# The last stage of a two-block network: half of a gather behind the first weight chunk, four scatter products split two and two

## The chip, the cores and the metric

One core of one Trainium2 chip. The time is that of the device from the first to the last instruction of the program, in microseconds (us). Names of engines: TensorE (PE in the profile; PEld is its weight load), VectorE (DVE), ScalarE (ACT), GpSimd (POOL), SyncE (SP), which here issues the weight transfers. 16 DMA engines move all data between the memory and the core.

## The reference, cut to what matters

The program runs a first block of two layers (mixers, cross attention, MLP) and then a second block. The change lies in the last part of the second, an expert-choice feed-forward network with 16 experts, each of which takes the 64 tokens of 512 that it rates highest:

```python
def expert_choice_ffn(h, w_router, b_router, w_gate, w_up, w_down):
    cap = (EC_CAPACITY_FACTOR * S) // N_EXPERTS          # 2 * 512 // 16 = 64
    affinity = jax.nn.softmax((h @ w_router + b_router).astype(jnp.float32), axis=-1)
    gates, idx = lax.top_k(affinity.transpose(0, 2, 1), cap)
    xin = h[bidx, idx]
    hid = jax.nn.silu(jnp.einsum('becd,edf->becf', xin, w_gate)) * jnp.einsum('becd,edf->becf', xin, w_up)
    y = jnp.einsum('becf,efd->becd', hid, w_down) * gates[..., None].astype(h.dtype)
    return jnp.zeros_like(h).at[bidx, idx].add(y)
...
x = x + gate2 * expert_choice_ffn(h2, w_router[l], b_router[l], w_gate[l], w_up[l], w_down[l])
```

The model width is 1024, an expert's inner width 2048, and everything is float32. The three weights of 16 experts are 403 MB.

## The kernel before, in words

Each engine has its own program, written out by hand; engines meet only at semaphores (`wait_ge`, `then_inc`), and an engine does its instructions in the order of its program. Where a text below says that something is queued behind a wait, that order is meant.

**Closing the mixer** (`close_parts`, from line 2480). The last output projection, the row scales, the router's logits and the ranks of the tokens are made. VectorE ends it with `hot` (L2717), a 0/1 matrix of tokens by slots for the first two experts, and signals `hot_ready`.

**The expert stage** (`experts`, from line 2724) works on experts in pairs, eight of them. Expert 0 of a pair uses columns 0 to 63 of TensorE's array and expert 1 columns 64 to 127. The weights come in chunks of 2048 KB (four blocks of 128 input features, 512 output columns, both experts), 24 for each pair: `per = 4 * nf + 8`, for each of the four quarters of the inner width two of the gate weight and two of the up weight, then eight of the down weight. The chunks of all pairs go through eight slots in turn (`slots`): four called ring, three in second_arena, one in hT. The first eight are loaded while the mixer is being closed. For every further chunk j SyncE waits until TensorE is through with chunk j - 8 (`tiles_done`) and then issues its load (L2785, L2786), in the order of the chunks.

On TensorE a pair is:

- `gather` (L2843): with `hot` it picks the 64 tokens of each expert out of `h2`, features in rows: 32 products of 128 columns, in two halves `q` of four feature blocks each, into bank 4 and bank 5; each half signals `s_gat`. VectorE moves each half to `xc` (`move_gathered`, L2929 to L2935, four instructions) and signals `s_x`.
- `pair_of_groups` (L2811): two chunks, with eight products each. Chunk q = 0 needs the first half of `xc`, q = 1 the second. In the first group of a pair TensorE waits for `s_x` ahead of each chunk (L2816).
- between the groups, one of the eight `scatter` products of the pair before (L2859), which bring its rows back to the tokens; for the first pair they work on zeros.
- turns of the hidden values, then the down projection, whose four groups are b = 0 (kg = 0, 1) for output columns 0 to 511 and b = 1 (kg = 0, 1) for 512 to 1023. The gather of the next pair comes after b = 0 (L2891).

The first pair's gather is called ahead of the loop (L2895), both halves in a row. The pairs 0 to 6 run in a loop (`Fori`), the last is written out.

**The end.** The last pair has no next pair under which its scatter products could go. The four of output half c = 0 are called by `scatter_half(0)` after kg = 0 of b = 1 (L2888, L2889), when two chunks are left; the four of c = 1 by `scatter_half(1)` at the very end (L2899). Each waits on `s_y`: VectorE has to multiply the down projection's result by gate2 first (L2981). VectorE's program for b = 0 and b = 1 is this, and it stays as it is:

```python
for b in range(2):
    dve.wait_ge(g.tiles_done, i * per + (base + 4 * nf + 4 * b + 4))
    nc.vector.tensor_tensor(y[:, b * BANK:b * BANK + BANK], g.psum[:, 6 + b, :],
                            gate2[:, b * BANK:b * BANK + BANK], ALU.mult).then_inc(s_y.up(), 1)
    if last:
        add_half(b)
```

`add_half(c)` (L2945) is four additions, one for each block of 128 tokens, each of which waits for its scatter product. SyncE and ScalarE write each finished block to the output (L2803, L2923). The last chunk of all is loaded in two halves (L2799), with a semaphore of its own for the second.

Of the kernel before, what the change touches and what calls it, by code (L numbers as in the profile page):

```python
# [12 lines left out]
P = 128  # L13
SEQ = 512
NT = SEQ // P
# [2708 lines left out]
def experts(g, ya, late, mod, gate2, out):  # L2724


    nc, t = g.nc, g.t
    pairs, nf = EXPERTS // 2, FE // BANK
# [20 lines left out]
    def preload(sp, which):  # L2749
        for s in which:  # L2750
# [4 lines left out]
    rows_ready, hot_ready, ya_turned, logits_done = opening[5:]  # L2755
    base = g.tiles
    primed = [g.counter("ex_" + n).up() for n in names for _ in range(2)]
    s_gat, s_x, s_silu, s_hid, s_turn, s_copy, s_y, s_back, s_add = (g.counter("ex_" + n) for n in names)
    all_primed = g.counter("built")
    s_gated, s_slots = g.counter("ex_slots_gated"), g.counter("ex_slots_turned")  # L2760
    xc, sg, y, h2, hot, gated, slot, aff, pos = (late[n] for n in ("xc", "sg", "y", "h2", "hot", "gated", "slot", "aff",
                                                                   "pos"))
# [3 lines left out]
    with nc.Block() as block:  # L2766
# [41 lines left out]
        def _(pe):  # L2808
            opening[2](pe)

            def pair_of_groups(i, j, bank, lhs, start, stop, halved=False, gathered=False):  # L2811

                for q in range(2):
                    w = ring[(j + q) % slots].rearrange("p (e k n) -> p e k n", e=2, k=half)
                    if gathered:
                        pe.wait_ge(s_x.sem, i * 2 + (s_x.base + q + 1))  # L2816
                    pe.wait_ge(landing[(j + q) % slots], i * (16 * per // slots) + landed_at[j + q])
                    for k in range(half):
                        if halved and q == 1 and k == half // 2:
                            pe.wait_ge(half_landed, 16)  # L2820
                        first, last = start and q == k == 0, stop and q == 1 and k == half - 1
                        for e in range(2):
                            mm = nc.tensor.matmul(g.psum[64 * e:64 * e + 64, bank, :],  # L2823
                                                  lhs(q * half + k)[:, 64 * e:64 * e + 64], w[:, e, k, :],
                                                  start=first, stop=last)
                    mm.then_inc(g.tiles_done, 1)
# [10 lines left out]
            def turn_slots(i):  # L2837
# [2 lines left out]
                    mm = nc.tensor.transpose(g.psum[:, 4, tt * P:tt * P + P], gated[:, tt, :], g.ident[:])  # L2840
                mm.then_inc(s_slots.up(), 1)

            def gather(i):  # L2843

                pe.wait_ge(hot_ready.sem, i + (hot_ready.base + 1))
                for q in range(2):
                    for k in range(4 * q, 4 * q + 4):
                        for tt in range(NT):
                            mm = nc.tensor.matmul(g.psum[:, 4 + q, (k % 4) * P:(k % 4) * P + P],  # L2849
                                                  h2[:, tt, k * P:k * P + P], hot[:, tt, :],  # L2850
                                                  start=(tt == 0), stop=(tt == NT - 1))
                    mm.then_inc(s_gat.up(), 1)

            def scatter(i, u):

# [3 lines left out]
                nc.tensor.matmul(g.psum[:, 6 + u % 2, :], sg[:, tt * P:tt * P + P], y[:, c * BANK:c * BANK + BANK],  # L2859
                                 start=True, stop=True).then_inc(s_back.up(), 1)  # L2860

            def scatter_half(c):

                pe.wait_ge(s_y.sem, (pairs - 1) * 2 + (s_y.base + c + 1))
                for tt in range(NT):
                    nc.tensor.matmul(g.psum[:, last_banks[c][tt], :], sg[:, tt * P:tt * P + P],  # L2866
                                     y[:, c * BANK:c * BANK + BANK], start=True, stop=True).then_inc(s_back.up(), 1)

            def pair(i, last):
                pe.wait_ge(s_y.sem, i * 2 + s_y.base)  # L2870
                for b in range(nf):
                    if b >= 2:
                        pe.wait_ge(s_hid.sem, i * nf + (s_hid.base + b - 1))
                    pair_of_groups(i, 4 * b, (b % 2) * 2, lambda k: xc[:, k, :], True, True, gathered=(b == 0))
                    scatter(i, 2 * b)
                    pair_of_groups(i, 4 * b + 2, (b % 2) * 2 + 1, lambda k: xc[:, k, :], True, True)
                    scatter(i, 2 * b + 1)
                    if b:
                        turn(i, b - 1)
                turn(i, nf - 1)  # L2880
                pe.wait_ge(s_copy.sem, i * nf + (s_copy.base + nf))
                turn_slots(i)
                pe.wait_ge(s_add.sem, i * 2 * NT + (s_add.base + 2 * NT))
                for b in range(2):
                    for kg in range(2):
                        pair_of_groups(i, 4 * nf + 4 * b + 2 * kg, 6 + b, lambda k: hT[:, kg * KD + k, :],
                                       kg == 0, kg == 1, last and b == kg == 1)
                        if last and b == 1 and kg == 0:  # L2888
                            scatter_half(0)  # L2889
                    if b == 0 and not last:  # L2890
                        gather(i + 1)  # L2891

            pe.wait_ge(*all_primed.at(1))
            pe.wait_ge(*rows_ready.at(NT))
            gather(0)  # L2895
            with pe.Fori(0, pairs - 1) as i:
                pair(i, False)
            pair(pairs - 1, True)
            scatter_half(1)  # L2899

        @block.scalar
# [192 lines left out]
```

## Time and profile before

| | us |
|---|---|
| median of 3 runs | 3101.69 |
| lowest and highest run | 3094.66 and 3102.46 |
| the profiled execution | 3105.4 |
| its span in the profile | 3103.7 |
| TensorE busy | 2888.8 (93%) |
| VectorE busy | 778.7 (25%) |
| ScalarE busy | 442.2 (14%) |
| mean DMA rate over the span | 184 GB/s |
| expert stage, from the first gather product (2173.17) to the end | 930.5 |

How to read the rows below. All times are us from the start of the span; a duration "mean ns" is in ns. In a **timeline** a row is: start, duration, engine, line of the kernel, operation, what it writes <- what it reads, shapes, count merged into the row, and in brackets the idle time of the engine before it and what ended that. Ends of products are modelled, so a row can end 0.1 us after the next one's start. TensorE does each float32 product in two passes, so a count is twice the number of products. In the **chain of waits** a row is: start, duration, and the engine, transfer or line that the end of the program hung on in that time. In a **table of stretches** a row is: from and to, length, busy us of PE, PEld, DVE, ACT and POOL with their instructions in brackets, the granted TensorE clock (1.00 is 2.4 GHz, 0.50 is 1.2 GHz), the busy share of the 16 DMA engines, and GB/s.

### The profile page before, as it was taken

The numbers are of one execution on the slowest core, as the hardware profiler recorded it, in microseconds if no ns is written. First come the engines' busy times: TensorE is split into PE (matmuls) and PEld (weight loads), VectorE is DVE, ScalarE is ACT, GpSimd is POOL, SyncE is SP. The second block draws the span as 40 slices with busy tenths as digits, with TensorE's granted clock in tenths as the row PEclk, the third lists the DMA queues.
The fourth block names the chain that finished last, engine by engine and source line by source line (L and its number), as shares of the span: only waits on it lengthen the run. The fifth ranks groups of instructions, "written<-read, shape, count | busy, mean of one in ns | idle before, by whom it ended". The sixth has DMA issues, their size and how long they took to land. (4 is left out here: it accounts for less than half of the span.)

```text
span 3103.7 us, 25172 instructions
## 1 busy us (share of the span) xinstructions
PE 2888.8 (93%) x9875; PEld 1323.0 (43%) x9875; DVE 778.7 (25%) x2032; ACT 442.2 (14%) x934; POOL 56.7 (2%) x149
## 2 busy tenths in 40 slices
PE   8998889999999999999999899798999899899888
PEld 4544544444444445444544444464433233233232
DVE  3398523101001214240000244544111111111111
ACT  2123412100001003211000122242000000000000
POOL 0000000000000000110000010000000000000000
PEclk9998999999999999999999999898999999999999
DMA  7230011212222111582112111213899999999998
GB/s 274 68 109 14 1 40 54 83 61 75 81 82 84 56 54 55 174 282 102 65 64 72 54 56 55 75 39 126 346 427 428 428 429 429 428 428 428 429 427 375
DMA packets 107475, 570.75 MB, mean 184 GB/s; under 512 B 11578, under 2 KB 12364, under 8 KB 82940
## 3 DMA queue, kind: packets, MB, share of 16 engines
q1 hardware_dynamic: 99248, 538.64, 43.2%
q0 software_dynamic: 6768, 29.43, 2.8%
q10 hardware_dynamic: 1372, 1.51, 0.1%
q8 instruction: 56, 0.92, 0.1%
q14 instruction: 31, 0.25, 0.0%
HBM read 567.43 MB, written 6.32 MB: 185 GB/s over the span
## 5 line engine op out<-in xcount | busy, mean ns | idle before, releaser
L205 PE MATMUL banks<-hT,ring 128*128 128x512 f32 x1024 | 441.5, 594 | 5.1 <-PEq L298 5.1
L205 PEld LDWEIGHTS banks<-hT,ring 128*128 128x128 f32 x1024 | 195.0, 191 | 250.4 <-issue 250.4
L2823 PE MATMUL banks<-ring,second_arena 128*64 128x512 f32 x1024 | 232.0, 597 | 29.7 <-DMA ring<-in_w_up 16.0
L1890 PE MATMUL banks<-ring,second_arena 128*128 128x512 f32 x512 | 222.6, 597 | 0.0
L324 PE MATMUL banks<-ring,m_u 128*128 128x512 f32 x512 | 220.3, 592 | 1.6 <-PEq L178 1.6
L2823 PE MATMUL banks<-second_arena 128*64 128x512 f32 x768 | 174.5, 598 | 17.4 <-DMA second_arena<-in_w_gate 15.0
L1890 PEld LDWEIGHTS banks<-ring,second_arena 128*128 128x128 f32 x512 | 98.2, 192 | 123.0 <-issue 123.0
L324 PEld LDWEIGHTS banks<-ring,m_u 128*128 128x128 f32 x512 | 97.0, 190 | 123.4 <-issue 123.4
L2823 PEld LDWEIGHTS banks<-ring,second_arena 128*64 128x64 f32 x1024 | 70.0, 136 | 184.0 <-issue 133.5
L2823 PE MATMUL banks<-ring,mod 128*64 128x512 f32 x512 | 114.7, 596 | 13.1 <-DMA ring<-in_w_down 13.1
L2943 DVE TENSOR_TENSOR x_rows<-banks,x_rows 128x512 f32<-128x512 f32 x64 | 44.2, 691 | 282.4 <-PE banks L2859 282.4
L1655 PE MATMUL banks<-hT,ring 128*128 128x512 f32 x256 | 112.1, 600 | 2.6 <-PEq L298 2.6
L1422 PE MATMUL banks<-ring,hT 128*128 128x512 f32 x256 | 111.1, 595 | 0.9 <-PEq L786 0.9
L2823 PEld LDWEIGHTS banks<-second_arena 128*64 128x64 f32 x768 | 51.2, 136 | 133.3 <-issue 89.6
L2823 PE MATMUL banks<-second_arena,mod 128*64 128x512 f32 x384 | 84.6, 595 | 2.5 <-DMA second_arena<-in_w_down 2.5
L2972 DVE TENSOR_TENSOR mod<-banks,mod 128x512 f32<-128x512 f32 x32 | 22.1, 691 | 244.4 <-PE banks L2823 244.4
L360 ACT ACTIVATE x_square<-x_rows 128x1024 f32<-128x1024 f32 x20 | 21.2, 1058 | 398.5 <-DVE x_rows L348 217.1
L1805 DVE SCALAR_TENSOR_TENSOR mod<-second_arena,mod 128x1536 f32<-128x1536 f32 x32 | 58.2, 1818 | 75.8 <-DMA second_arena<-in_w_ada 75.7
L1655 PEld LDWEIGHTS banks<-hT,ring 128*128 128x128 f32 x256 | 49.1, 192 | 64.1 <-issue 64.1
L1422 PEld LDWEIGHTS banks<-ring,hT 128*128 128x128 f32 x256 | 48.7, 191 | 62.0 <-issue 61.2
L2823 PE MATMUL banks<-hT,second_arena 128*64 128x512 f32 x256 | 58.3, 597 | 14.9 <-DMA hT<-in_w_up 14.9
L2859 PE MATMUL banks<-second_arena 128*128 128x512 f32 x128 | 72.0, 645 | 0.0
(578 smaller groups left out, 3027.7 us busy)
## 6 DMA issues: line engine op xcount, KB each, us to landing
ring<-in_w_up SPq DMA_DIRECT2D x48, 2048.0 KB, 30.7
ring<-in_w_down SPq DMA_DIRECT2D x48, 2048.0 KB, 33.8
ring<-in_w_gate SPq DMA_DIRECT2D x32, 2048.0 KB, 34.0
second_arena<-in_w_gate SPq DMA_DIRECT2D x32, 2048.0 KB, 30.7
second_arena<-in_w_down SPq DMA_DIRECT2D x24, 2048.0 KB, 35.4
second_arena<-in_w_up SPq DMA_DIRECT2D x16, 2048.0 KB, 32.4
hT<-in_w_up SPq DMA_DIRECT2D x16, 2048.0 KB, 33.8
second_arena<-in_w_ada POOLq DMA_DIRECT2D x32, 768.0 KB, 4.8
```

What stands on the lines that cost most here:

```text
L205: mm = nc.tensor.matmul(o, w[:, k, a:z], src[:, ka, 0:ntok], start=(ka == 0), stop=(ka == kc * kgroups - 1))
L324: mm = nc.tensor.matmul(g.psum[:, b * NT + m, :], act[:, ka, m * P:m * P + P], w[:, k, :], start=(ka == 0), stop=(ka == kc * kgroups - 1))
L360: g.alink(nc.scalar.activation(square[:], g.x[:, t, :], ACT.Square, accum_out=g.row_stats[:, 0, t:t + 1]))
L1422: mm = nc.tensor.matmul(bank, a[:, k, m * P:m * P + P], w[:, k, :], start=(k == 0), stop=(k == kc - 1))
L1655: mm = nc.tensor.matmul(o, w[:, k, m * P:m * P + P], g.hT[:, k, :], start=(k == 0), stop=(k == KD - 1))
L1805: nc.vector.scalar_tensor_tensor(o, w[:, n % 2, :], cs[:, k:k + 1], o, ALU.mult, ALU.add).then_inc(added.up(), 1)
L1890: mm = nc.tensor.matmul(g.psum[:, b * NT + m, :], u[:, ka, m * P:m * P + P], w[:, k, :], start=(ka == 0), stop=(ka == KD * kgroups - 1))
L2823: mm = nc.tensor.matmul(g.psum[64 * e:64 * e + 64, bank, :], lhs(q * half + k)[:, 64 * e:64 * e + 64], w[:, e, k, :], start=first, stop=last)
L2859: nc.tensor.matmul(g.psum[:, 6 + u % 2, :], sg[:, tt * P:tt * P + P], y[:, c * BANK:c * BANK + BANK], start=True, stop=True).then_inc(s_ba ...
L2943: nc.vector.tensor_tensor(xs, g.psum[:, 6 + u % 2, :], xs, ALU.add).then_inc(s_add.up(), 1)
L2972: nc.vector.tensor_tensor(hid[:, b % 2, :], g.psum[:, (b % 2) * 2 + 1, :], act_g[:, b % 2, :], ALU.mult).then_inc(s_hid.up(), 1)
```

## The change

Two edits, both in TensorE's program. The other engines' programs are as before.

1. The gather is cut into `gather_half(q)`. The first pair is taken out of the loop and written out. Ahead of it only `gather_half(0)` is done; `gather_half(1)` comes inside its first group, after the products of chunk 0 and ahead of the wait for the second half of `xc`. Pairs 1 to 6 run in the loop as before, and their gathers are as before.
2. In the last pair, `scatter_half(0, ...)` is called twice: token blocks 0 and 1 after kg = 0 of b = 1 and token blocks 2 and 3 after kg = 1, that is after the last chunk.

```diff
                 for q in range(2):
                     w = ring[(j + q) % slots].rearrange("p (e k n) -> p e k n", e=2, k=half)
+                    if gathered and q and isinstance(i, int) and i == 0:
+                        gather_half(1)
                     if gathered:
                         pe.wait_ge(s_x.sem, i * 2 + (s_x.base + q + 1))
                     pe.wait_ge(landing[(j + q) % slots], i * (16 * per // slots) + landed_at[j + q])
...
+            def gather_half(q):
+                for k in range(4 * q, 4 * q + 4):
+                    for tt in range(NT):
+                        mm = nc.tensor.matmul(g.psum[:, 4 + q, (k % 4) * P:(k % 4) * P + P],
+                                              h2[:, tt, k * P:k * P + P], hot[:, tt, :],
+                                              start=(tt == 0), stop=(tt == NT - 1))
+                mm.then_inc(s_gat.up(), 1)
+
             def gather(i):
 
                 pe.wait_ge(hot_ready.sem, i + (hot_ready.base + 1))
                 for q in range(2):
-                    for k in range(4 * q, 4 * q + 4):
-                        for tt in range(NT):
-                            mm = nc.tensor.matmul(g.psum[:, 4 + q, (k % 4) * P:(k % 4) * P + P],
-                                                  h2[:, tt, k * P:k * P + P], hot[:, tt, :],
-                                                  start=(tt == 0), stop=(tt == NT - 1))
-                    mm.then_inc(s_gat.up(), 1)
+                    gather_half(q)
...
-            def scatter_half(c):
+            def scatter_half(c, tiles=range(NT)):
 
                 pe.wait_ge(s_y.sem, (pairs - 1) * 2 + (s_y.base + c + 1))
-                for tt in range(NT):
+                for tt in tiles:
...
-                        if last and b == 1 and kg == 0:
-                            scatter_half(0)
+                        if last and b == 1:
+                            scatter_half(0, (2 * kg, 2 * kg + 1))
                     if b == 0 and not last:
                         gather(i + 1)
 
             pe.wait_ge(*all_primed.at(1))
             pe.wait_ge(*rows_ready.at(NT))
-            gather(0)
-            with pe.Fori(0, pairs - 1) as i:
+            pe.wait_ge(*hot_ready.at(1))
+            gather_half(0)
+            pair(0, False)
+            with pe.Fori(1, pairs - 1) as i:
                 pair(i, False)
             pair(pairs - 1, True)
             scatter_half(1)
```

## Rows read from the trace of the kernel before

**Rows 1.** Table of stretches, the first and a late 100 us of the stage.

```profile
2182.00:2282.00 100.00, 99.19 (x474) 38.03 (x475) 14.97 (x28) 5.95 (x9) 0.00 (x0) 1.00 0.96 405
2982.00:3082.00 100.00, 85.51 (x366) 26.70 (x364) 9.68 (x14) 5.95 (x9) 0.00 (x0) 1.00 1.01 428
```

**Rows 2.** Chain of waits, where it turns to the transfers, and one round.

```profile
2334.25 32.40 DMA ring<-in_w_down
2366.69 3.68 PE banks L2823 x16
2370.39 35.44 DMA ring<-in_w_up
2405.87 3.68 PE banks L2823 x16
```

**Rows 3.** Timeline of the opening: gather, its two moves, first products.

```profile
2173.17 9.27 PE L2849 MATMUL banks<-second_arena 128*128 128x128 f32 x64 [1.46 <-DVE second_arena L2717]
2179.01 1.37 DVE L2933 TENSOR_SCALAR second_arena<-banks,mod_columns 128x128 f32<-128x128 f32 x4 [5.98 <-PE banks L2849]
2182.37 7.09 PE L2823 MATMUL banks<-ring,second_arena 128*64 128x512 f32 x32
2182.48 1.36 DVE L2933 TENSOR_SCALAR second_arena<-banks,mod_columns 128x128 f32<-128x128 f32 x4 [2.10 <-PE banks L2849]
```

**Rows 4.** Timeline of SyncE's queue: the first, the second and the third refill.

```profile
2186.07 0.33 SPq L2786 DMA_DIRECT2D ring<-in_w_gate  x1
2189.50 0.33 SPq L2786 DMA_DIRECT2D ring<-in_w_gate  x1
2194.14 3.76 SPq L2786 DMA_DIRECT2D ring<-in_w_up  x2
```

**Rows 5.** Table of stretches, single microseconds: clock, and bytes after the first refill.

```profile
2177.00:2178.00 1.00, 1.00 (x10) 1.00 (x10) 0.00 (x0) 0.00 (x0) 0.00 (x0) 0.94 0.00 0
...
2186.00:2187.00 1.00, 1.00 (x8) 0.29 (x5) 0.00 (x0) 0.00 (x0) 0.00 (x0) 1.00 0.00 0
2187.00:2188.00 1.00, 1.00 (x6) 0.29 (x4) 0.00 (x0) 0.00 (x0) 0.00 (x0) 1.00 1.16 246
2188.00:2189.00 1.00, 1.00 (x8) 0.29 (x4) 0.00 (x0) 0.00 (x0) 0.00 (x0) 1.00 0.82 344
```

**Rows 6.** Timeline of the second pair's gather and its first move.

```profile
2264.06 7.41 PE L2849 MATMUL banks<-second_arena 128*128 128x128 f32 x64
...
2267.93 1.36 DVE L2933 TENSOR_SCALAR second_arena<-banks,mod_columns 128x128 f32<-128x128 f32 x4 [3.07 <-PE banks L2849]
```

**Rows 7.** Timelines of TensorE, then VectorE, in the last 25 us.

```profile
3081.69 3.65 PE L2823 MATMUL banks<-second_arena,mod 128*64 128x512 f32 x16 [1.24 <-DMA second_arena<-in_w_down]
3085.27 3.70 PE L2866 MATMUL banks<-second_arena 128*128 128x512 f32 x8
3088.90 3.65 PE L2823 MATMUL banks<-second_arena,mod 128*64 128x512 f32 x16
...
3096.78 3.70 PE L2866 MATMUL banks<-second_arena 128*128 128x512 f32 x8 [0.79 <-DVE second_arena L2981]
...
3086.44 0.69 DVE L2950 TENSOR_TENSOR x_rows<-banks,x_rows 128x512 f32<-128x512 f32 x1 [10.15 <-PE banks L2866]
3087.29 0.69 DVE L2950 TENSOR_TENSOR x_rows<-banks,x_rows 128x512 f32<-128x512 f32 x1 [0.17 <-PE banks L2866]
...
3096.04 0.69 DVE L2981 TENSOR_TENSOR second_arena<-banks,mod 128x512 f32<-128x512 f32 x1 [6.34 <-PE banks L2823]
```

**Rows 8.** Timeline of TensorE: two pauses of earlier stages.

```profile
462.65 15.67 PE L1103 MATMUL banks<-hT,ring 128*128 128x512 f32 x32 [2.55 <-PEq L298]
...
1787.62 27.70 PE L2083 MATMUL banks<-hT,ring 128*128 128x512 f32 x64 [1.67 <-PEq L1848]
```

**Rows 9.** Table of stretches, around and behind these two pauses.

```profile
1786.00:1790.00 4.00, 2.38 (x6) 1.22 (x7) 1.69 (x4) 1.07 (x2) 0.00 (x0) 1.00 0.72 218
463.00:468.00 5.00, 5.00 (x9) 2.06 (x8) 1.82 (x12) 0.00 (x0) 0.00 (x0) 0.66 0.54 207
```

## The prediction

> **What bounds the kernel now.** The change touches two places, the opening of the expert stage and its last 20 us, so I read first what connects them. In the table of 100 us stretches the 16 DMA engines are full from the first expert chunk to the last: 428 GB/s at a share of 1.01 near the end, and 405 GB/s in the first stretch, which is what is left of 428 if nothing moves for its first 5 us [rows 1]. In the chain of waits the stage is one pattern, 3.68 us of products, then 35.44 us of a transfer, again and again [rows 2]: a slot is released, its new chunk is queued behind seven others, lands, and is used. One round is 2405.87 - 2366.69 = 39.18 us for eight slots, so 39.18 / 8 = 4.90 us per chunk of 2048 KB, 428 GB/s. TensorE needs less: two chunks in a row are 3.43 us apart and with a scatter product between them 4.64 us [rows 4]. So the **weight stream sets the end**. It starts when the first of the eight preloaded slots is released, and whatever moves its start, or makes a hole in it, moves the end by as much. A hole elsewhere on TensorE costs nothing while it has chunks in store. At the very end the order turns round: after the last chunks have landed TensorE, VectorE and the write of the output are in line, and there each microsecond counts again.
>
> The sum is made against the profiled execution, 3105.4 us with a span of 3103.7. That is 3.7 us above the median of the runs, 3101.69; I carry the difference over to the median. The runs themselves lie 7.8 us apart (3094.66 to 3102.46), more than anything below. About 0.3%, 9.3 us, is what a measurement of this kernel can tell from no change.
>
> **The opening, part by part.** Before: both halves of the gather start at 2173.17 and take 9.27 us; VectorE moves the first half from 2179.01 for 1.37 us, under the second half, and the first chunk starts at 2182.37 without waiting for anything [rows 3]. SyncE issues the first refill at 2186.07, that is 3.70 us later, and the second at 2189.50 [rows 4].
>
> After, the first half still ends for VectorE at 2179.01 (the clock's cold part lies all in it: 0.94 is granted in the microsecond from 2177 [rows 5], and the change touches nothing ahead of that). Now nothing lies beside the move: 2179.01 + 1.37 = 2180.38, a hand-over of 0.07, first chunk at 2180.45, its release and the first refill at 2180.45 + 3.70 = **2184.15, 1.92 us earlier**. This is the gain, and it is real.
>
> Then the second half of the gather stands on TensorE between chunk one and chunk two. At full clock a half costs what it costs in the second pair, 3.87 us from the start of the gather to VectorE's first move [rows 6]; starting at about 2183.98 it is there at 2187.85. The move behind it takes 1.36 us and is now bare as well (before it ran under the first chunk): 2189.21, hand-over 0.07, second chunk at 2189.28, second refill at 2189.28 + 3.70 = **2192.98, 3.48 us later** than before.
>
> What does the stream make of that? Before, the second transfer was queued at 2189.50 but its turn came only when the first was through, as if issued at 2186.07 + 4.90 = 2190.97; the 1.47 us between were cover. After, the first transfer is alone and is through at the equivalent of 2184.15 + 4.90 = 2189.05, and the second is issued at 2192.98. The engines stand idle for 3.9 us, and the second and every later chunk is 2192.98 - 2190.97 = **2.0 us later**. The early refill gives one chunk a head start and takes it back from all the others. The third refill follows 4.64 us after the second [rows 4], at 2197.62, against a need at 2192.98 + 4.90 = 2197.88: 0.26 us of cover, then more with each chunk (3.43 and 4.64 in turn against 4.90). So there is one hole and not a row of them. After a pause the engines also have to get going again: no bytes in the microsecond after the first refill's issue, 246 GB/s in the next and 344 in the one after it [rows 5]. The latency to the first byte is the same in both kernels and cancels; of the ramp I add the last part, (428 - 344) / 428 = 0.2 us; its bounds are 0 and 0.6 us (with the 246 as well). It can't be below nothing, since a transfer that starts from rest isn't faster than one in a full queue. **Opening: +2.2 us, between +1.9 and +2.8.**
>
> The rest of the opening is free. TensorE is about 3.5 us later through the first pair, which only eats into its store of landed chunks: the chain is on TensorE until 2334 and goes to a transfer only there, 150 us on [rows 2]. If that store were gone, it would cost these 3.5 us. The first pair leaves the loop and stands as straight code; its instructions are as many, and entry to the loop moves to a place with the same cover. Queued on VectorE behind its longer wait for the second half is the gating of the slots, which is needed only after all sixteen up and gate chunks. On SyncE nothing is moved but the times of the issues.
>
> **The tail.** Before, TensorE finishes the last but two chunk, does the four products of the first output half (3085.27 to 3088.90, so 3.63 us: 1.06 for the first and 0.857 for each further), then the last two chunks, after which VectorE multiplies (3096.04) and the second four products start at 3096.78 [rows 7]. The weights' own time would be earlier: chunk 190 lands 4.90 us after chunk 189, whose products start at 3081.69, so at 3086.59, and is used at 3088.90.
>
> After, only two products stand before the last two chunks: 2 x 0.857 = 1.71 us less, chunk 190 starts at 3087.19, still 0.6 us behind its landing. The last group ends 1.71 us earlier and the two remaining products start where its successor would stand. VectorE follows a last product by 0.11 (2182.37 to 2182.48 [rows 3]), so that place was 3096.04 - 0.11 = 3095.93 and is 1.71 less now, 3094.22. But VectorE works in the order of its program, and that isn't changed: all four additions of the first half, and only then the multiplication of the second half, on which the last four products wait. The first addition starts 3086.44 - 3085.27 = 1.17 us after the first product [rows 7], so the third addition now starts at 3095.39, the fourth 0.85 later (3086.44 to 3087.29) at 3096.24, ends 0.69 later at 3096.93, and the multiplication starts there instead of at 3096.04. Everything behind it (0.7 us multiplication, products, additions, a write) is as before. **Tail: +0.9 us.** The 1.7 us of product time are taken off the path ahead of the last chunks, and 1.17 + 0.85 + 0.69 = 2.7 us of product and additions are put on it behind them. What can add: the last chunk has to land up to 1.7 us earlier than it was wanted, and the output writes of the first half (128 x 512 floats, 256 KB, 0.6 us each at 428 GB/s) share the engines with it; two of the four are now behind it. I put that at 0, with a bound of +0.5. Nothing in the order on VectorE leaves room below +0.9.
>
> **Sum: 2.2 + 0.9 = +3.1 us.** The profiled execution would be 3108.5, the median 3101.69 + 3.1 = **3104.8 us**, which is within 0.3%.
>
> **The rivals.** *The gains stand.* The head start of 1.92 us would reach the end if the second refill came by 2189.05, and the tail would gain if the multiplication weren't behind the additions: the last products would then start when the two before them are through, at 3094.22 + 1.06 + 0.86 = 3096.14 instead of 3096.78, 0.64 us earlier. Together -2.6 (1.92 + 0.64), 3099.1 us. Against it stand the 3.87 + 1.36 us between the chunks and the order in the code; for it only that landing and issue times may be looser than I read them. 7%.
>
> *The clock falls in the new pauses* (the case that ends clearly slower). TensorE is idle for 1.6 us before the first chunk and for 1.4 us before the second. Rows on both sides: after a pause of 1.67 us the granted clock stayed at 1.00, its upper level of 2.4 GHz, while after one of 2.55 us the next 5 us ran at 0.66 on the mean [rows 8, 9], which is (1 - 0.66) x 5 = 1.7 us lost. New pauses are nearer to the first. One fall puts the second refill 1.7 us later, two 3.4: +4.8 or +6.5, 3106.5 to 3108.2 us; 7%. It would pass 9.3 us only if the clock stayed at 0.50 for both chunks and the half between them, 3.6 + 3.6 us more and so +10.3, 3112 us; 2%. The Trainium skill (TensorE: Matmul & The Clock Gate, HAM oscillation) speaks against this change here: bursts of products with pauses between them can throw the clock back to half rate again and again. By that rule the time would be the dearer of these cases; the row of 1.67 us is why I don't take it.
>
> *The change does nothing*: the stream's start doesn't set the end, say because a later place refills the queue. 3101.7 us, give or take the tail. The table of stretches shows no gap in which the stream could be caught up [rows 1]; 4%.
>
> **How the numbers follow.** Forecast 80%, and the rivals 7, 7, 2 and 4%. The costs themselves span +2.8 to +4.2 us (1.9 + 0.9 to 2.8 + 1.4); the wider part of the range is from the runs, whose median may fall 4 us to either side, and more below, where one run of before lies 7 us under the two others. 3097.5 to 3109.5 us takes in every case but the last clock case. Faster by over 0.3% would need a median under 3092.4: 2%. Slower by over 0.3%, above 3111: the full clock case and an unlucky spread, 4%. Within 0.3%: 94%.
>
> **What would show it.** In the changed kernel's trace: first refill 1.9 us earlier after the start of the gather and second 3.5 us later; a pause without bytes of 3 to 4 us between them; chunk-to-chunk times of 4.90 as before; the whole stage from the start of the gather to the last chunk's products some 2.2 - 1.7 = 0.5 us longer; at the end two additions between the last group and the multiplication, which starts 2.7 us after that group instead of at once. Wrong is the prediction if the engines are busy through the pause, if the clock reads under 1.00 at 2180 to 2193, or if the multiplication comes ahead of the third addition.

## The result

The changed kernel takes 3107.22 us, median of 21 runs (3098.27 to 3109.96), against 3103.01 us for the kernel before in the 21 runs beside it, which include the three shown above. The ratio is 1.0019 with a 95% interval of 1.0011 to 1.0027, that is 3.4 to 8.4 us: a little slower, by less than the 0.3% that is told from no change here. The forecast was 3104.8 us, +3.1.

The profiled execution has a span of 3106.9 us, 3.2 above the 3103.7 of before. Its chain of waits, at the opening and at the end (start, duration, what the end of the program hung on):

```profile
2172.79 5.70 PE banks L2848 x32
2178.48 1.61 issue
2180.09 3.65 PE banks L2825 x16
2183.75 3.78 PE banks L2848 x32
2187.88 1.05 DVE second_arena L2940 x3
2188.97 3.65 PE banks L2825 x16
...
3084.11 3.65 PE banks L2825 x16
3087.76 1.91 PE banks L2871 x4
3089.68 7.02 PE banks L2825 x32
3096.69 1.93 PE banks L2871 x4
3098.65 0.69 DVE x_rows L2957
3099.34 0.61 DVE second_arena L2988
3099.99 3.71 PE banks L2871 x8
```

Lines have moved: L2825 is the product of a weight chunk (L2823 before), L2848 the gather, L2871 the scatter of the last pair, L2957 and L2988 the addition and the multiplication on VectorE. Beside [rows 3] a pause now follows each half of the gather, and the second half stands between two chunks. Beside [rows 7] there is an addition between the last group of products and the multiplication.

SyncE's queue, the first three refills:

```profile
2183.78 0.33 SPq L2786 DMA_DIRECT2D ring<-in_w_gate  x1
...
2192.67 0.33 SPq L2786 DMA_DIRECT2D ring<-in_w_gate  x1
2197.31 0.33 SPq L2786 DMA_DIRECT2D ring<-in_w_up  x1
```

Counted from the first gather product (2173.17 before, 2172.79 now), the first refill comes at 10.99 instead of 12.90 us and the second at 19.88 instead of 16.33 [rows 4]. The hole between them in the table of stretches, by single microseconds (the last three columns are clock, share of the DMA engines, GB/s):

```profile
2184.00:2185.00 1.00, 1.00 (x11) 1.00 (x10) 0.00 (x0) 0.00 (x0) 0.00 (x0) 1.00 0.73 164
2185.00:2186.00 1.00, 1.00 (x11) 1.00 (x10) 0.00 (x0) 0.00 (x0) 0.00 (x0) 1.00 0.67 180
2186.00:2187.00 1.00, 1.00 (x11) 1.00 (x10) 0.00 (x0) 0.00 (x0) 0.00 (x0) 1.00 1.00 426
...
2190.00:2191.00 1.00, 1.00 (x8) 0.32 (x6) 0.00 (x0) 0.00 (x0) 0.00 (x0) 1.00 0.05 16
2191.00:2192.00 1.00, 1.00 (x6) 0.29 (x4) 0.00 (x0) 0.00 (x0) 0.00 (x0) 1.00 0.06 16
2192.00:2193.00 1.00, 1.00 (x5) 0.30 (x2) 0.00 (x0) 0.25 (x1) 0.00 (x0) 1.00 0.00 0
2193.00:2194.00 1.00, 1.00 (x4) 0.20 (x4) 0.19 (x1) 1.00 (x1) 0.00 (x0) 1.00 0.87 180
2194.00:2195.00 1.00, 1.00 (x8) 0.33 (x6) 0.50 (x1) 0.63 (x2) 0.00 (x0) 1.00 0.54 197
2195.00:2196.00 1.00, 1.00 (x8) 0.39 (x6) 0.00 (x0) 0.00 (x0) 0.00 (x0) 1.00 0.95 410
```

The first transfer goes through alone, then three microseconds move next to nothing, and a second start from rest follows. These stretches are cut at whole microseconds and not at the issue, so they can't be set beside [rows 5]. Counted from the issue, the first two microseconds of each start are these: first the kernel before, then the first and the second start of the changed kernel.

```profile
2186.07:2187.07 1.00, 1.00 (x6) 0.29 (x4) 0.00 (x0) 0.00 (x0) 0.00 (x0) 1.00 0.40 82
2187.07:2188.07 1.00, 1.00 (x8) 0.35 (x6) 0.00 (x0) 0.00 (x0) 0.00 (x0) 1.00 0.76 164
...
2183.78:2184.78 1.00, 1.00 (x9) 1.00 (x10) 0.00 (x0) 0.00 (x0) 0.00 (x0) 1.00 0.34 82
2184.78:2185.78 1.00, 1.00 (x11) 1.00 (x10) 0.00 (x0) 0.00 (x0) 0.00 (x0) 1.00 1.02 246
...
2192.67:2193.67 1.00, 1.00 (x4) 0.24 (x5) 0.00 (x0) 0.92 (x1) 0.00 (x0) 1.00 0.35 82
2193.67:2194.67 1.00, 1.00 (x7) 0.43 (x8) 0.69 (x1) 0.96 (x2) 0.00 (x0) 1.00 0.79 180
```

Each start has the same two slow microseconds, and the third is at 426, 328 and 393 GB/s. TensorE is busy through nearly the whole hole (1.00 in each microsecond from 2190): nothing in its own row would tell that anything is lost there. The clock reads 1.00 on both sides of the new pauses.

### The profile page after: what moved, and what is told of

It is laid out like the page before. It is cut to its first block and busy times, and to the rows that moved or that the text cites. A ratio compares the mean times of both kernels' runs of the same rounds, so it can differ in the third digit from the quotient of the medians.

```text
span 3106.9 us, 25150 instructions
## 1 busy us (share of the span) xinstructions
PE 2889.2 (93%) x9875; PEld 1324.9 (43%) x9875; DVE 778.2 (25%) x2032; ACT 442.2 (14%) x934; POOL 57.2 (2%) x149
## 3 DMA queue, kind: packets, MB, share of 16 engines
q10 hardware_dynamic: 1372, 1.51, 0.2%
## 5 line engine op out<-in xcount | busy, mean ns | idle before, releaser
L2825 PE MATMUL banks<-ring,second_arena 128*64 128x512 f32 x1024 | 232.2, 598 | 32.8 <-DMA ring<-in_w_up 16.0
L2825 PE MATMUL banks<-second_arena 128*64 128x512 f32 x768 | 174.5, 598 | 17.3 <-DMA second_arena<-in_w_gate 15.0
L2825 PEld LDWEIGHTS banks<-ring,second_arena 128*64 128x64 f32 x1024 | 70.1, 136 | 186.6 <-issue 134.5
L2825 PE MATMUL banks<-ring,mod 128*64 128x512 f32 x512 | 114.7, 596 | 12.4 <-DMA ring<-in_w_down 12.4
L2825 PEld LDWEIGHTS banks<-second_arena 128*64 128x64 f32 x768 | 51.2, 136 | 133.2 <-issue 89.9
L2825 PE MATMUL banks<-second_arena,mod 128*64 128x512 f32 x384 | 84.6, 595 | 2.5 <-DMA second_arena<-in_w_down 2.5
L2825 PE MATMUL banks<-hT,second_arena 128*64 128x512 f32 x256 | 58.3, 597 | 14.9 <-DMA hT<-in_w_up 14.9
```

The source lines that it names most:

```text
L2825: mm = nc.tensor.matmul(g.psum[64 * e:64 * e + 64, bank, :], lhs(q * half + k)[:, 64 * e:64 * e + 64], w[:, e, k, :], start=first, stop=last)
```

## How the experiments are read

Runs of one and the same kernel lie some 12 us apart (3093.66 to 3105.69 for the kernel before), far more than the terms in question. One reason shows long ahead of the stage. A pause of TensorE and the 7 us from its end, in the kernel before:

```profile
1005.38 7.08 PE L1655 MATMUL banks<-hT,ring 128*128 128x512 f32 x12 [2.55 <-PEq L298]
...
1005.40:1012.40 7.00, 7.00 (x13) 3.02 (x14) 3.31 (x17) 0.00 (x0) 0.60 (x16) 0.76 0.54 192
```

and the same place in e10 below, a second execution of the same kernel:

```profile
1002.92 7.11 PE L1655 MATMUL banks<-hT,ring 128*128 128x512 f32 x16 [2.55 <-PEq L298]
...
1003.00:1010.00 7.00, 7.00 (x18) 3.17 (x19) 3.26 (x17) 0.00 (x0) 0.54 (x15) 1.00 0.54 193
```

Behind the same pause of 2.55 us the clock fell in one execution (0.76 over 7 us, so (1 - 0.76) x 7 = 1.7 us lost) and not in the other. Of the thirteen traces here five have the fall at this place and eight don't. The kernel before has it at the like pauses at 556 and 1184 us as well (0.77 over 7 us each), and e10 at neither. Mostly by such falls the two executions of one kernel are 2173.17 - 2168.60 = 4.57 us apart by the start of the gather. So each trace is split at that start. **A** is from the first gather product to the start of the products of the last chunk but two (3081.69 - 2173.17 = 908.52 before), **B** from there to the end of the last addition (3101.21 - 3081.69 = 19.52). Between, the refills are counted from the first gather product too; there are 184, and the numbers below are the difference to the kernel before at the 1st, 2nd, 61st, 171st and last one. Worked out from the rows of SyncE's queue and of TensorE:

```
                       refill 1      2     61    171    184       A        B
before                     0.00   0.00   0.00   0.00   0.00   908.52   19.52
e10 before again          -0.16  -0.15  -0.18  -0.19  -0.19   908.33   19.52
after                     -1.91  +3.55  +2.85  +2.78  +2.80   911.32   20.31
e9  after again           -1.92  +3.54  +1.96  +1.88  +3.10   911.61   20.31
e1  opening alone         -1.92  +3.55  +2.50  +2.48  +3.64   912.16   19.53
e8  written out alone     -0.16  -0.16  -0.40  -0.39  +0.81   909.41   19.52
e4  short half            -1.92  +0.87  +0.08  +0.06  +0.31   908.85   19.53
e5  double half           -1.92  +7.11  +6.65  +6.61  +7.06   915.59   19.53
e6  four firsts           -2.06  -2.06  -2.49  -2.48  -0.91   907.59   19.53
e2  end alone             -0.02  -0.02  -0.15  -0.23  -0.21   908.31   20.31
e3  end mended            -0.02  -0.01  -0.10  -0.14  -0.14   908.40   18.65
e7  both mended           -2.06  -2.05  -2.37  -2.37  -0.91   907.60   18.66
e11 both mended again     -1.91  -1.91  -2.24  -2.23  -0.76   907.76   18.66
```

B repeats to 0.01 us for each form of the end. The stream's position repeats to 0.4 us for the kernels with no hole, and to 0.9 for those with one.

## The two edits alone

**e1** has the opening of the changed kernel and the end of the one before:

```diff
-                        if last and b == 1:
-                            scatter_half(0, (2 * kg, 2 * kg + 1))
+                        if last and b == 1 and kg == 0:
+                            scatter_half(0)
```

> The opening as changed (half of the gather behind the first chunk, first pair written out), the end as before. Measured in the trace as two stretches: A from the start of the first gather product to the start of the products of the last chunk but two (908.5 us before, 911.3 with the whole change), and B from there to the end of the last addition (19.5 before, 20.3 with the whole change). Stream theory (a hole in the weight stream is paid at the end in full): A 911.3, B 19.5, so 2.8 us above the kernel before. Rival 1 (the head start is kept and the loss is made elsewhere, in the end): A 906.6, B 19.5, 1.9 us below. Rival 2 (the two edits cost more together than alone, since the writes of the output meet the last chunk): A 911.3 but B under 19.5 or over 20.

A 912.16, B 19.53; ratio 1.0010 (0.9998 to 1.0023). The loss is in A as the stream theory has it, and B is that of before, so the head start isn't kept and the edits don't meet. Up to refill 171 it is +2.5. The rest, 1.15 us, comes in one jump at refill 173, which no theory had foreseen; it has a section of its own below.

**e2** is the kernel before with the split scatter products alone (`scatter_half` takes the token blocks as in the change).

```diff
...
-                        if last and b == 1 and kg == 0:
-                            scatter_half(0)
+                        if last and b == 1:
+                            scatter_half(0, (2 * kg, 2 * kg + 1))
```

> The end as changed (two scatter products before the last two chunks, two behind), the opening as before. Stretch A 908.5, B 20.3 (+0.8) if VectorE's order is the cost: the second multiplication starts 2.7 us behind the start of the two late products. Rival (the end costs nothing by itself and its 0.8 us come from the late stream): A 908.5, B 19.5 or less.

A 908.31, B 20.31; ratio 1.0006 (0.9996 to 1.0016). The whole +0.8 of the end is there without the late stream.

**e3** keeps that split and gives VectorE the order that would suit it:

```diff
...
                     if last:
-                        add_half(b)
+                        add_half(0, (2 * b, 2 * b + 1))
+                    if last and b == 1:
+                        add_half(1)
```

(with the multiplication of b = 1 ahead of it, and `add_half` taking the token blocks it is to add).

> As the run with the end alone, and VectorE's order changed too: two additions, then the second multiplication, then the other two additions and the last four. Theory (the cost of the end is VectorE's order, not the products): the multiplication starts 0.1 us behind the last group again, the last four products follow the two late ones without a pause, B is 19.5 - 0.65 to 19.5 - 0.85 = 18.7 to 18.9. Rival (the last chunk's landing is what ends last once the products are out of the way): the last group ends no earlier than before and B stays at 19.5 or above.

B 18.65, inside what was expected, if at its favourable edge; ratio 1.0002 (0.9992 to 1.0012), so the gain shows in the trace alone. The timeline of its end:

```profile
3090.14 3.60 PE L2823 MATMUL banks<-hT,mod 128*64 128x512 f32 x16
3093.67 5.42 PE L2866 MATMUL banks<-second_arena 128*128 128x512 f32 x12
3093.79 0.69 DVE L2981 TENSOR_TENSOR second_arena<-banks,mod 128x512 f32<-128x512 f32 x1 [6.33 <-PE banks L2823]
3094.83 0.69 DVE L2950 TENSOR_TENSOR x_rows<-banks,x_rows 128x512 f32<-128x512 f32 x1 [0.35 <-PE banks L2866]
```

and the changed kernel's:

```profile
3093.09 3.60 PE L2825 MATMUL banks<-hT,mod 128*64 128x512 f32 x16
3096.62 1.98 PE L2871 MATMUL banks<-second_arena 128*128 128x512 f32 x4
3097.79 0.69 DVE L2957 TENSOR_TENSOR x_rows<-banks,x_rows 128x512 f32<-128x512 f32 x1 [7.38 <-PE banks L2871]
3098.65 0.69 DVE L2957 TENSOR_TENSOR x_rows<-banks,x_rows 128x512 f32<-128x512 f32 x1 [0.17 <-PE banks L2871]
3099.26 0.68 DVE L2988 TENSOR_TENSOR second_arena<-banks,mod 128x512 f32<-128x512 f32 x1
3099.99 3.70 PE L2871 MATMUL banks<-second_arena 128*128 128x512 f32 x8 [1.38 <-DVE second_arena L2988]
```

From the start of the two late products the multiplication comes after 0.12 us in e3 and after 2.64 us in the changed kernel. In e3 all six products are one group without a pause. The order on VectorE alone turns a gain of 0.87 us (19.52 - 18.65) into a loss of 0.79; the products as split are a gain.

## Is it the hole?

**e4** and **e5** leave the first refill where the change puts it and move only the second, by changing how long the second half of the gather takes.

```diff
-            def gather_half(q):
-                for k in range(4 * q, 4 * q + 4):
-                    for tt in range(NT):
+            def gather_half(q, tiles=NT, times=1):
+                for k in list(range(4 * q, 4 * q + 4)) * times:
+                    for tt in range(tiles):
...
-                        gather_half(1)
+                        gather_half(1, tiles=1)      # e4; e5: times=2
```

Both have the end of the kernel before. e4 leaves out 12 of the 16 products of that half, so its output isn't that of the network; it serves for its times alone.

> The opening as changed, the end as before, and of the first pair's second gather half only 4 of 16 products are done (the first token block of each feature block; the rest is left out, so the first pair gets incomplete features in blocks 4 to 7). The half takes 0.95 instead of 3.8 us, so the second refill comes 2.85 us earlier, 17.0 us behind the start of the gather; the first at 11.0. Stream theory: lateness of the second refill against the turn it had before (12.9 + 4.9 = 17.8) is -0.8, plus the 0.7 us of a second start from rest that the changed kernel showed over its 2.1 us of lateness: A = 908.5 - 0.8 + 0.7 = 908.4, or 907.7 if the hole is too small for a second start. Rival (every microsecond of hole costs its length, whatever the head start): the hole is 17.0 - 15.9 = 1.1 us, A = 908.5 + 1.1 = 909.6. Rival (the first refill alone sets the stream): A = 906.6.

> The opening as changed, the end as before, and the first pair's second gather half is done twice over (the same products into the same bank, so no value changes). It takes 3.7 us more, so the second refill is at 19.9 + 3.7 = 23.6 us behind the start of the gather. Stream theory: A grows by the same 3.7 us over the run with the opening alone, 911.3 + 3.7 = 915.0, the 0.7 us of the second start from rest being paid once. Rival (the store of landed chunks hides it, and the 2.8 us of the change come from elsewhere, as the written-out pair): A stays at 911.3.

e4: the second refill is at 17.20 us (16.33 + 0.87) and the stream is +0.08 at refill 61. The bound by turn, 12.90 + 4.90 = 17.80, is undercut by 0.60, and 0.68 that come on top take it back. The hole is 17.20 - 10.98 - 4.90 = 1.3 us long, so the rival that charges the hole's whole length is out by 1.2 us, and the one by which the first refill alone counts by 2.0. A is 908.85, 0.45 above the expected 908.4; 0.25 of that is a late jump again. Its timed ratio, 1.0010 (1.0000 to 1.0020), is more than this trace explains: the traced run, at 3103.20 us, was the lowest of its eight (up to 3106.86), and their medians lie 3.2 us apart. That stays open, and what is read from e4 is read from one trace.

e5: the second refill at 23.44 (16.33 + 7.11), 3.56 later than in e1; the stream at refill 61 is +6.65, which is 4.15 above e1 and 3.80 above the changed kernel. Lateness against the turn is 23.44 - 17.80 = 5.64, and 1.0 comes on top. A 915.59, 0.6 above the forecast, 0.4 of which is a late jump; ratio 1.0025 (1.0014 to 1.0035). Lateness goes through to the end one to one; the store of chunks hides none of it.

So the stream's shift is the second refill's lateness against its old turn (-0.60, +2.08, +5.64) plus something: +0.08 + 0.60 = 0.7 in e4; 2.85, 2.50 and 1.96 less 2.08, so 0.8, 0.4 and -0.1, in the three traces with the change's opening; 1.0 in e5. It is 0.6 on the mean of the five, and differs from run to run by half a microsecond either way.

The time from issue to landing (the last figure, in us) shows where it is lost, and that it isn't the second start itself. The first, second and third refill of the changed kernel:

```profile
ring<-in_w_gate SPq DMA_DIRECT2D x1, 2048.0 KB, 7.7
ring<-in_w_gate SPq DMA_DIRECT2D x1, 2048.0 KB, 7.3
ring<-in_w_up SPq DMA_DIRECT2D x1, 2048.0 KB, 8.7
```

The first refill of the kernel before takes 7.7 us too, so the second start is as quick as a first one: when the second refill lands, the five traces are 0.1 to 0.3 us ahead of the lateness of its issue. The third was issued 4.64 us after the second and took 8.66 us instead of 7.34, so it landed 5.96 us after it and not 4.90. In the five traces with a hole this distance is 5.8 to 6.7 us, in the eight without one 4.9 to 5.0. Single late transfers come without a hole as well: the sixth refill is 0.8 to 0.9 us late in the kernel before, e2, e3, e8 and e10. From the landing of the second refill to that of the 61st the five lose 0.2 to 1.2 us more than the kernel before does, 0.8 on the mean, and 0.8 less the 0.2 is the 0.6. So what comes on top is a difference between single late transfers. That the third one goes with the hole is clear, five of five against none of eight; what delays it isn't shown.

**e6** tries whether the head start can be kept if there is no hole. The first eight chunks come in another order, so that four of them need only the first half of the features:

```diff
     def source(i, j):
+        if isinstance(i, int) and i == 0 and j < slots:
+            return (wg, wu)[j % 2][0, 2 * ((j // 2) % 2) + j // 4]
...
+            def first_chunks():
+                for j in range(slots):
+                    q, bank = j // 4, j % 4
+                    w = ring[j].rearrange("p (e k n) -> p e k n", e=2, k=half)
+                    if j == 3:
+                        gather_half(1)
+                    if bank == 0:
+                        pe.wait_ge(s_x.sem, s_x.base + q + 1)
+                    pe.wait_ge(landing[j], landed_at[j])
...
+                    if q:
+                        scatter(0, bank)
+                turn(0, 0)
```

(and ScalarE and VectorE wait in the first pair for the chunks at which gate and up are now complete).

> End as before. First pair written out, its first eight chunks in another order: the first-half chunks of gate and up of two quarters (four chunks, four banks), then the four second-half chunks. Only half of the gather ahead of chunk one; the second half stands between the third and the fourth chunk and its move is under the fourth. Stream theory: releases at 11.0, 14.6, 18.2, 25.7 us behind the start of the gather against needs of 11.0, 15.9, 20.8, 25.7, so no hole, and the head start of 1.9 us reaches the end: A = 908.5 - 1.9 = 906.6; up to 0.7 more if the fourth comes too late by a little. Rival (the written-out pair or the early refill costs by itself): A 908.5 or more.

There is no hole (compare the hole shown above; here are ten microseconds each):

```profile
2180.00:2190.00 10.00, 10.00 (x62) 5.89 (x58) 0.00 (x0) 0.00 (x0) 0.00 (x0) 1.00 0.98 385
2190.00:2200.00 10.00, 10.00 (x46) 3.24 (x46) 2.66 (x6) 1.88 (x2) 0.00 (x0) 1.00 1.00 426
```

The releases come at 10.84, 14.27, 17.71 and 25.07 us, the fourth 0.5 us ahead of its need (10.84 + 3 x 4.90 = 25.54), and for the whole middle of the stage the stream is 2.5 us ahead of before. A is still only 907.59, -0.9: 1.56 us go at refill 173, at one stroke. Ratio 0.9999 (0.9990 to 1.0008). The stream theory holds up to there, and the forecast for A was wrong for another reason.

**e7** is e6 with the mended end of e3.

> The opening with four first-half chunks and the end with VectorE's order changed. If both theories hold the two gains add up: A 906.6, B 18.7 to 18.9, 2.6 us below the kernel before in all, 0.08%, ratio about 0.999. Rival (the gains meet: the earlier end of the products finds the last chunk not landed): A 906.6, B 19.5, 1.9 us below.

A 907.60, B 18.66: the end's gain is there in full beside the other, 0.92 + 0.86 = 1.8 us by the trace; median 3100.84 against 3102.86, ratio 0.9993 (0.9983 to 1.0002). Its second set of runs, e11, gives 0.9996 (0.9987 to 1.0006). It is the best of the kernels here by its traces, and not told from the kernel before by its times.

## The jump in the last pair

By then five traces had one jump of 0.2 to 1.6 us somewhere in the last pair, which consists of chunks 168 to 191 (the text of e8 gives the first of them wrongly as 176), and all five had the first pair written out. e8 does only that:

```diff
             gather(0)
-            with pe.Fori(0, pairs - 1) as i:
+            pair(0, False)
+            with pe.Fori(1, pairs - 1) as i:
                 pair(i, False)
```

> As the kernel before, but the first pair is taken out of TensorE's loop and written out; the gather stays whole and in front, the end as before. The steady stream was once held up by 0.2 to 1.6 us, always during the last pair (chunks 176 to 191), in five of the traces whose first pair is written out, and in none of the three where it is in the loop (before, end alone, end mended). Theory (the written-out pair moves where instruction blocks are fetched, and a fetch during the last pair holds up the stream): the releases run level with those of the kernel before (within 0.2 us) up to the last pair and then lose 0.2 to 1.6 us; A 908.7 to 910.1. Rival (the hold-ups are chance, or come with the shifted stream): A 908.5.

> The changed kernel once more, for a second trace of it. Its first trace shows no hold-up in the last pair and A 911.3. If hold-ups come and go with the run, this one may show one of 0.2 to 1.6 us, A 911.5 to 912.9; if they are fixed by where the code lies, none, A 911.3 again. The releases up to the last pair should be +2.5 to +2.9 us against the kernel before in either case.

> The kernel before once more, for a second trace of it: A 908.5 and B 19.5 if its stream is never held up in the last pair; up to 910.1 if the hold-ups are chance.

> The kernel with four first-half chunks and the mended end once more. Releases 2.4 us ahead of the kernel before up to the last pair. If the hold-up is fixed by where the code lies it comes back at the same chunk with 1.4 to 1.6 us (A 907.6, B 18.7); if it is chance, A is 906.1 and the whole 3.2 us below the kernel before.

e8 runs 0.4 us ahead of before up to refill 171 and ends at +0.81: a jump of 1.2 us, A 909.41; ratio 1.0000 (0.9991 to 1.0010). e10, the kernel before again, has none, A 908.33. e11 has it at refill 173 with 1.47 us, as e1, e6 and e7 (1.15, 1.56, 1.43). e9 is the changed kernel, whose first trace has no jump at all, and here one at refill 180 that leaves 1.2 us, at the same place as e8; so A is 911.61 in place of the 911.3 that a fixed place would have given, while its stream before the jump is only at +1.9. Its ratio is 1.0010 (1.0001 to 1.0020).

Taken together: eight of nine traces with the first pair written out have a jump (0.24, 0.42 and six from 1.15 to 1.56 us), none of four without. As far as thirteen traces can tell, it goes with writing the pair out, though it comes in the last pair, 800 us behind the copy. It isn't fixed by the code alone, since one kernel shows it in one trace and not in the other. What does it isn't settled. TensorE waits for a chunk that lands late; in e8:

```profile
3023.14 3.65 PE L2823 MATMUL banks<-ring,second_arena 128*64 128x512 f32 x16 [0.18 <-DMA ring<-in_w_up]
3029.36 5.26 PE L2823 MATMUL banks<-ring,second_arena 128*64 128x512 f32 x16 [2.57 <-DMA ring<-in_w_up]
```

and in the two microseconds from 3026 the DMA queues hold, beside the weights, one block of instructions:

```profile
q8 instruction: 1, 0.02, 3.2%
```

3.2% of 16 engines for 2 us is 1.0 us of one engine, about the size of the jump, and in e1, e6, e7, e8, e9 and e11 such a read lies within the 4 us ahead of the late chunk's products. The page counts 56 such blocks where the pair is in the loop and 59 or 60 where it is written out. The opening has a case of the same kind: four traces (e5, e6, e7, e11) read a block 2.5 us ahead of the first refill's landing, and there it takes 8.5 to 8.9 us to land, against 7.3 to 8.0 in the nine others, which read theirs ahead of its first bytes or in its last 0.6 us. But e4 and e5 have no read so close to their small jumps, the kernel before reads three blocks in the last pair and loses nothing, and the changed kernel's first trace has two reads there, each about 1 us ahead of a landing, and no jump. A read that falls on the DMA engine that is the last one anyway would fit all of this; which engine a block goes to wasn't seen, so that stays an argument.

## Why the prediction was right, and where not

- **First refill 1.92 us earlier**: 1.91 in both traces. Second 3.48 later: 3.55 and 3.54. Each step of that sum (the move bare, 3.87 for the half, 3.70 from a chunk's start to its refill) held to 0.1 us.
- **The hole is paid by all later chunks**, 2.0 us: 2.08 against the turn, and e4 and e5 show the slope of one.
- **The second start from rest**, 0.2 with bounds 0 and 0.6: the measured extra is -0.1 to 1.0, 0.6 on the mean of five traces. This is the term that was mis-sized, and its reason was wrong too. The ramp cancels as the latency does, since the kernel before starts from rest as well and the turn of its second transfer is counted from there; by the landing of the second refill the second start has cost nothing extra (0.1 to 0.3 us less than nothing). What came on top came behind it, first with the third refill, landed 5.96 instead of 4.90 us after the second, and the sum had no term for single late transfers. That its size is near the term's upper bound is chance. The opening as a whole was +2.2 (1.9 to 2.8) and measured 2.85, 2.50 and 1.96 by the middle of the stage.
- **The tail**, +0.9: measured 0.79 in each of three traces. The mechanism (VectorE's order) is shown by e3. The 0.1 us are the overlap of the multiplication with the addition ahead of it (3098.65 + 0.69 = 3099.34, started at 3099.26), against my sentence that nothing leaves room below 0.9. The possible +0.5 for the last chunk's landing didn't come: TensorE's last group ran on without a gap, and in e3 and e7 too.
- **The clock** stayed at 1.00 through pauses of 1.61 and 1.46 us, as the row of 1.67 us had said [rows 8, 9], and did so in all five traces with these two pauses; the dearer rival fell. Two rows could not carry more than that, though. The same pause of 2.55 us is followed by a fall in one execution and by none in another, as shown above, and a pause of 1.51 us among small products at 2155 us of the kernel before has the clock at 0.50 from 2157 on. The Trainium skill (TensorE: Matmul & The Clock Gate, HAM oscillation) says that bursts with waits for transfers between them can bring the clock down again and again; the waits of its case are longer than these two pauses, so it did not speak as clearly against the change as the prediction has it. A longer wait does come in this stage: the jump in e8 makes a pause of 2.57 us, and behind it the clock reads 0.56 and 0.50 and the chunk takes 5.26 instead of 3.65 us.
- **"The first pair ... written out ... its instructions are as many"**, costed at nothing: wrong, by the traces. It costs nothing at its own place (e8 is level with before there and at refill 171), but e8's A is 0.9 to 1.1 us above the two traces of before, through the jump (by its times, ratio 1.0000, this isn't seen). It was left out because I asked only what the copy does where it stands, and not what shifts behind it.
- **The sum**, +3.1: by traces A and B together are +2.80 + 0.79 = +3.6 and +3.09 + 0.79 = +3.9. What came behind the second start, and in e9 the jump, make up the difference. The timed ratios are 1.0019 and 1.0010, so +5.9 and +3.1 us. The first of them is held up by the kernel before: six of its 21 runs lie between 3093.6 and 3094.7 us and one of the changed kernel's at 3098.3. In the runs beside e1 there are six of that kind (four of the kernel before, two of e1), each with a granted clock of 0.980 or 0.981 over the span where all others have 0.975 to 0.979; this fits a clock that was down for less time, and both kernels have them. By medians the two sets give 4.2 and 3.7 us. The stated range, 3097.5 to 3109.5 us, would have held a kernel without any change as well (3103.01 us), so that the median fell into it says little; the two intervals above 1.000 and the positions in the traces bear the forecast out.

```profile
3029.00:3031.00 2.00, 1.64 (x4) 0.53 (x6) 0.00 (x0) 0.00 (x0) 0.00 (x0) 0.56 0.96 410
3031.00:3032.00 1.00, 1.00 (x6) 0.26 (x4) 0.00 (x0) 0.00 (x0) 0.00 (x0) 0.50 1.08 459
3032.00:3033.00 1.00, 1.00 (x6) 0.35 (x4) 0.00 (x0) 0.00 (x0) 0.00 (x0) 0.68 0.89 377
```

(The clock behind the pause of e8, table of stretches; third column from the end.)

## What to carry to other kernels

Where a stream of transfers sets the end, ask of each edit at its start not when the first slot is released but whether slot n is released by the time that the first n - 1 transfers take: the latest of these sets the stream, and a head start for one transfer alone is lost in the hole behind it. Work split over two places of one engine has to be split on the engine that answers it as well, or the early wait of one becomes the late start of the other. And to tell a few microseconds in a kernel whose runs lie ten apart, count from a landmark inside the trace.

## What was not expected of the hardware

A weight stream that starts from rest, with its queue empty, moved 16 to 82 GB/s in the first microsecond from the issue and 164 to 246 in the second (the first start of each trace), against 428 in the steady stream, and a second start in the same stage was no dearer than the first: 2 MB landed after 7.3 to 7.5 us in all five traces that have one, and after 7.3 to 8.9 at the first start. The transfer behind the second start was late by 0.9 to 1.8 us each time. A stream that was steady to 0.1 us over 110 transfers lost up to 1.6 us on a single chunk, near the read of a 16 KB block of instructions, in code that had only been moved. And a pause of TensorE of 2.55 us, the same in every execution, was followed by the clock's fall to its lower level in five executions of thirteen and by none in the other eight.
